# Norm sums and spreads as transposes, a down projection that ends bank by bank, and a last norm in two token halves

## The reference

```
def rmsnorm(x, g):
    y = x * lax.rsqrt(jnp.mean(x * x, axis=-1, keepdims=True) + EPS)
    return y * g
# first_block, for l in 0, 1:
    y = concat(diff_attention, spatial_gating, window_gqa)(rmsnorm(x, g_pre_mix) @ w_in) @ w_out
    x = x + rmsnorm(y, g_post_mix)
    f = (silu(h @ gate) * (h @ up)) @ w_ffn_out          # h = rmsnorm(x, g_pre_ffn)
    x = x + rmsnorm(f, g_post_ffn)
    e = p @ w_ple_up;  g = sigmoid(rmsnorm(x, g_ple_gate) @ w_ple_gate)
    x = x + rmsnorm(e * g, g_ple_post)
# second_block, for l in 0, 1:
    x = x + 0.5 * swiglu(norm(x)); x = x + mixer(norm(x)); x = x + 0.5 * swiglu(norm(x))
return norm(x)
```

## Time and profile before

| | us |
|---|---|
| median of 3 runs (3361.12 to 3364.63) | 3361.33 |
| the profiled execution, its own time | 3360.54 |
| its span in the trace | 3358.7 |
| TensorE matmul busy | 3292.1 (98%) |
| GpSimd busy | 1647.3 (49%) |
| VectorE, ScalarE busy | 1176.9, 1171.3 (35% each) |

### The profile page before, as it was taken

How to read it: one execution, slowest core, us unless ns; L and a number is a source line. 1 busy time by engine, 2 the same in 40 slices (tenths; PEclk the granted TensorE clock), 3 DMA queues, 4 the chain that set the end, 5 groups by cost and what they waited for, 6 DMA issues and landing times.

```text
span 3358.7 us, 44116 instructions
## 1 busy us (share of the span) xinstructions
PE 3292.1 (98%) x16096; PEld 2719.8 (81%) x16096; DVE 1176.9 (35%) x1850; ACT 1171.3 (35%) x1852; POOL 1647.3 (49%) x906
## 2 busy tenths in 40 slices
PE   8999999999999999999999999999999999999998
PEld 6788888787788887888888788888888887688887
DVE  4534124445441144511344332124311443321133
ACT  4744222448442233422233442223322233332232
POOL 6735444567254445644456244444544452354443
PEclk9999999999999999999999999999999999999998
DMA  4112222231122222322222112222222221122221
GB/s 151 45 47 99 94 100 94 69 110 45 38 95 100 94 100 75 117 95 99 94 88 101 51 69 93 95 96 98 97 95 99 94 95 69 63 94 94 98 96 57
DMA packets 80800, 293.87 MB, mean 87 GB/s; under 512 B 8971, under 2 KB 9355, under 8 KB 80428
## 3 DMA queue, kind: packets, MB, share of 16 engines
q1 hardware_dynamic: 79344, 286.06, 24.4%
q10 hardware_dynamic: 1340, 6.23, 0.5%
HBM read 290.15 MB, written 2.10 MB: 87 GB/s over the span
## 4 chain that ended last, share of the span: by engine, by line
PE 89%; POOL 4%; DVE 3%; issue 3%; ACT 1%; DMA 0%; POOLq 0%; SPq 0%; DVEq 0%; ACTq 0%
PE bank L1989 28%; PE bank L1991 27%; PE bank L1990 27%; POOL w_lo L559 1%; PE bank L2436 1%; POOL diag L698 1%; POOL scr L617 1%; PE bank L2397 1%; PE bank L2417 1%; PE bank L2035 1%; PE bank L2259 0%; PE bank L2017 0%; DVE y L1601 0%; PE bank L2237 0%; POOL small L611 0%
## 5 line engine op out<-in xcount | busy, mean ns | idle before, releaser
L559 POOL TENSOR_TENSOR w_lo<-w_raw,w_hi 128x1024 fp32r<-128x1024 f32 (+1 forms) x541 | 1307.4, 2420 | 1501.4 <-ACT w_hi L789 1501.2
L1989 PE MATMUL bank<-mvh,w_hi 128*128 128x512 f32 (+1 forms) x4520 | 1739.7, 385 | 31.5 <-DVE mvl L1303 14.4
L1991 PE MATMUL bank<-mvh,w_lo 128*128 128x512 f32 (+1 forms) x4520 | 1714.9, 379 | 0.0
L1990 PE MATMUL bank<-mvl,w_hi 128*128 128x512 f32 (+1 forms) x4520 | 1714.5, 379 | 0.0
L789 ACT ACTIVATE w_hi<-w_raw 128x1024 fp32r<-128x1024 f32 x537 | 568.5, 1060 | 1752.3 <-PE bank L1991 1748.7
L1989 PEld LDWEIGHTS bank<-mvh,w_hi 128*128 128x128 f32 x4520 | 851.9, 188 | 221.5 <-issue 40.5
L1991 PEld LDWEIGHTS bank<-mvh,w_lo 128*128 128x128 f32 x4520 | 851.7, 188 | 161.7
L1990 PEld LDWEIGHTS bank<-mvl,w_hi 128*128 128x128 f32 x4520 | 852.4, 189 | 152.7 <-issue 0.2
L1412 DVE TENSOR_TENSOR scr<-bank,rstd_b 128x512 f32<-128x512 f32 x264 | 181.3, 690 | 994.4 <-PE bank L1991 994.2
L1429 DVE TENSOR_TENSOR mvl<-big,mvh 128x512 fp32r<-128x512 f32 x132 | 269.3, 2050 | 347.4 <-ACT mvh L916 347.4
L698 POOL TENSOR_TENSOR diag<-diag,scr 128x512 f32<-128x512 f32 (+1 forms) x137 | 153.9, 1123 | 24.1 <-ACT scr L804 12.7
(11 more groups left out here) (195 smaller groups left out, 1565.2 us busy)
## 6 DMA issues: line engine op xcount, KB each, us to landing
w_raw<-in_weights SPq DMA_DIRECT2D x537, 512.0 KB, 3.2
x<-in_x SPq DMA_DIRECT2D x8, 256.0 KB, 8.0
out_y<-y SPq DMA_DIRECT2D x4, 512.0 KB, 2.7
tab<-in_dist ACTq DMA_DIRECT2D x2, 640.0 KB
tab<-in_gmlp ACTq DMA_DIRECT2D x2, 640.0 KB
tab<-in_ret_dil ACTq DMA_DIRECT2D x1, 1280.0 KB
y<-in_p ACTq DMA_DIRECT2D x2, 512.0 KB, 3.7
y<-in_rotary ACTq DMA_DIRECT2D x1, 1024.0 KB
```

What stands on the lines that cost most here:

```text
L559: last = nc.gpsimd.tensor_tensor(w_lo[:, slot, at], w_raw[:, slot, at], w_hi[:, slot, at].bitcast(F32), ALU.subtract)
L1989: nc.tensor.matmul(bank[:, at], hi, mvh[:, k, at], start=first, stop=False)
L1990: nc.tensor.matmul(bank[:, at], hi, mvl[:, k, at], start=False, stop=False)
L1991: return nc.tensor.matmul(bank[:, at], lo, mvh[:, k, at], start=False, stop=last)
```

## The change

Four things are changed.

1. `sum_squares` transposes the summed squares instead: four transposes of 128x128 fill bank STAT (for a half two, and two more of the last square), and DVE adds up along the free axis with a new `reduce_sum` ahead of the variance. `spread` transposes too. Each of these is one instruction for a block where there were two.
2. In `a_ffn_out` the last two units are worked bank by bank: both units' products for bank 2, then for bank 0, and so on. The norm is no longer in `DIRECT`: POOL adds all eight squares, begins with them ahead of `w_lo` of the gate's first unit, and makes that unit between the last add and the root. ACT makes `w_hi` of the last units behind the squares, and `w_hi` of the gate's third unit ahead of the first `moving_from_x` tile. The sum moves from behind the third `ple_tile` to behind the second.
3. `b_post_out1` ends bank by bank as well, and in two token halves: first all eight banks for tokens 0 to 255, then for 256 to 511 in the order of `LAST_ORDER`, with 256-column matmuls.
4. The final norm is done for each half by itself. The sum and the spread of the first half stand between matmuls of the second; y is stored in eight DMAs of 256 KB.

```diff
+LAST_ORDER = (tuple(range(8)), (1, 5, 0, 2, 3, 4, 6, 7))
...
-        DIRECT = {"final": 5}
+        DIRECT = {"final": KT - 1}
         for l in range(LAYERS):
-            DIRECT.update({f"a_out{l}": KT - 1, f"a_ffn_out{l}": KT - 1, f"a_ple{l}": KT - 1})
+            DIRECT.update({f"a_out{l}": KT - 1, f"a_ple{l}": KT - 1})
...
+        TWO_STEPS = SPLIT_POST + ["final"]
...
             return sq[:, k % 4, part(half)]
+
+        def turned(name, half):
...
-            for k in range(0, KT, 2):
-                sp.wait_ge(y_ready, k + 2)
-                sp.dma_start(y_out[:, k:k + 2, :], y[:, k:k + 2, :]).then_inc(out_stored, 16)
-            sp.wait_ge(out_stored, 16 * (KT // 2))
+            for half in range(2):
+                for k in range(0, KT, 2):
+                    sp.wait_ge(y_ready, KT * half + k + 2)
+                    sp.dma_start(y_out[:, k:k + 2, HALF[half]], y[:, k:k + 2, HALF[half]]).then_inc(out_stored, 16)
+            sp.wait_ge(out_stored, 16 * KT)
...
+                splits(u0)
+                add_squares(f"a_ffn_out{l}", 0, KT)
                 splits(u0 + 1)
-                add_squares(f"a_ffn_out{l}", 0, KT - 1)
                 root(f"a_ffn_out{l}")
                 splits(u0 + 2)
...
-            add_squares("final", 0, DIRECT["final"])
-            root("final")
+            add_squares("final", 0, KT - 1)
+            add_squares("final", KT, KT + 3)
+            root("final", 0)
+            add_squares("final", KT + 3, KT + KT - 1)
...
                     if gate and 1 <= k <= 4:
                         take_e(int(name[-1]), k + 3)
-                    if gate and k in (1, 5):
-                        after_unit(lin[f"a_ple_up{name[-1]}"], 0, k // 5)
+                    if gate and k == 5:
...
-                ffn_out(f"a_ffn_out{l}", f"a_ffn_in{l}")
+                ffn_out(f"a_ffn_out{l}", f"a_ffn_in{l}", tail=2)
...
                     square(f"a_ffn_out{l}", n, banks[BACK[n]][:, :])
+                after_unit(lin[f"a_ffn_out{l}"], 0, FT - 2)
                 after_unit(lin[f"a_ffn_out{l}"], 0, FT - 1)
                 for n in range(4):
                     take_e(l, n)
+                after_unit(lin[f"a_ple_up{l}"], 0, 0)
...
                 ffn_out(f"b_post_out{l}", f"b_post_in{l}", tail=4 if l else 0)
-            for k in range(KT):
-                act.wait_ge(x_ready, XR["b_post1"] + k + 1)
-                square("final", k, x[:, k, :])
+            for i in range(2 * KT):
+                act.wait_ge(x_ready, XR["b_post1"] + i + 1)
...
+                if turned(name, half):
+                    src = var4[:, at]
+                    if half is None:
+                        chain(nc.vector.reduce_sum(src, banks[STAT][:, :].rearrange("p (b c) -> p b c", c=P), AX.X))
+                    else:
+                        chain(nc.vector.reduce_sum(src, banks[STAT][:, :].rearrange("p (a b c) -> p b a c", a=2, c=P),
+                                                   AX.XY))
+                nc.vector.tensor_scalar(var4[:, at], src, 1.0 / D, EPS, ALU.mult, ALU.add).then_inc(var_ready, 1)
 
...
+            def last_sum(half, j):
+
+                at, k = HALF[half], LAST_ORDER[half][j]
+                dve.wait_ge(last_out, KT * half + j + 1)
+                nc.vector.scalar_tensor_tensor(out=x[:, k, at], in0=banks[BACK[k]][:, at], scalar=0.5,
+                                               in1=x[:, k, at], op0=ALU.mult, op1=ALU.add).then_inc(x_ready, 1)
+
+            def output(half, k):
+
+                at = HALF[half]
+                if k == 0:
+                    spread_ready("final", half)
+                nc.vector.scalar_tensor_tensor(out=y[:, k, at], in0=x[:, k, at], scalar=col("final", k),
+                                               in1=banks[STAT if half else BCAST][:, at], op0=ALU.mult,
+                                               op1=ALU.mult).then_inc(y_ready, 1)
+
             for k in range(KT):
-                update(k)
-            rstd_ready("final")
+                last_sum(0, k)
             for k in range(KT):
-                nc.vector.scalar_tensor_tensor(out=y[:, k, :], in0=x[:, k, :], scalar=col("final", k),
-                                               in1=banks[BCAST][:, :], op0=ALU.mult,
-                                               op1=ALU.mult).then_inc(y_ready, 1)
+                if k == 3:
+                    variance("final", 0)
+                last_sum(1, k)
+                if k == 6:
+                    output(0, 0)
+            for k in range(1, KT):
+                if k == 3:
+                    variance("final", 1)
+                output(0, k)
+            for k in range(KT):
+                output(1, k)
 
 
         @block.tensor
         def _(pe):
-            def three(bank, slot, tile, k, first, last, half=None):
+            def three(bank, slot, tile, k, first, last, half=None, again=False):
 
                 hi, lo = w_hi[:, slot, tile * P:(tile + 1) * P], w_lo[:, slot, tile * P:(tile + 1) * P]
                 at = part(half)
-                nc.tensor.matmul(bank[:, at], hi, mvh[:, k, at], start=first, stop=False)
-                nc.tensor.matmul(bank[:, at], hi, mvl[:, k, at], start=False, stop=False)
-                return nc.tensor.matmul(bank[:, at], lo, mvh[:, k, at], start=False, stop=last)
+                nc.tensor.matmul(bank[:, at], hi, mvh[:, k, at], start=first, stop=False, skip_group_check=again)
+                nc.tensor.matmul(bank[:, at], hi, mvl[:, k, at], start=False, stop=False, skip_group_check=again)
+                return nc.tensor.matmul(bank[:, at], lo, mvh[:, k, at], start=False, stop=last, skip_group_check=again)
 
             def wide(name):
...
                 pe.wait_ge(sq_used, used(name, end - (KT - first)))
+                if turned(name, half):
+                    if NORM[name] == 0:
+                        pe.wait_ge(consts, 16)
+                    for j, b in enumerate(bs):
+                        last = nc.tensor.transpose(banks[STAT][:, j * P:(j + 1) * P], diag[:, b, :], ident[:, :])
+                    if half is not None:
+                        pe.wait_ge(sq_ready, base + end)
+                        for j in range(2):
+                            last = nc.tensor.transpose(banks[STAT][:, (2 + j) * P:(3 + j) * P],
+                                                       sq_at(name, end - 1)[:, j * P:(j + 1) * P], ident[:, :])
+                    last.then_inc(sums_done, 1)
+                    return
                 for b in bs:
                     last = nc.tensor.matmul(banks[STAT][:, b:b + 1], diag[:, b, :], ones[:, 0:1], start=(b == bs[0]),
                                             stop=(first == KT), skip_group_check=True)
...
-                    last = nc.tensor.matmul(banks[STAT if half else BCAST][:, b * P:(b + 1) * P], rstd4[:, b:b + 1].broadcast_to([P, P]),
-                                            ident[:, :], start=True, stop=True)
+                    last = nc.tensor.transpose(banks[STAT if half else BCAST][:, b * P:(b + 1) * P],
+                                               rstd4[:, b:b + 1].broadcast_to([P, P]), ident[:, :])
...
                         body(t, 2 + j)
-                for f in range(FT - 4, FT):
+                if name[0] == "b" and name != "b_post_out1":
+                    for f in range(FT - 4, FT):
+                        body(0, f)
+                    return
+                for f in (FT - 4, FT - 3):
                     body(0, f)
+                pe.wait_ge(w_lo_ready, L.u0 + FT)
+                pe.wait_ge(mv_lo, L.m0 + FT)
+                if name == "b_post_out1":
+                    last_outputs(L)
+                    return
+                for n in range(8):
+                    for f in (FT - 2, FT - 1):
+                        last = three(banks[BACK[n]], (L.u0 + f) % RING, n, f % 4, False, f == FT - 1)
+                        if n == 7:
+                            last.then_inc(unit_done, 1)
+                    if n < 7:
+                        last.then_inc(out_done, 1)
+
+            def last_outputs(L):
+
+                for half in range(2):
+                    for j in range(KT):
+                        n = LAST_ORDER[half][j]
+                        if half:
+                            pe.wait_ge(x_ready, XR["b_post1"] + n + 1)
+                        for f in (FT - 2, FT - 1):
+                            last = three(banks[BACK[n]], (L.u0 + f) % RING, n, 4 + f % 4, False, f == FT - 1, half, half == 1)
+                        last.then_inc(last_out, 1)
+                        if half and j == 2:
+                            pe.wait_ge(x_ready, XR["b_post1"] + KT + 2)
+                            sum_squares("final", 0)
+                        if half and j == 5:
+                            spread("final", 0)
+                sum_squares("final", 1)
+                spread("final", 1)
 
             def ple_tile(l, n):
...
 
```

(19 more changed lines are left out.)

13 lines of the change are left out of this document (9 added, 4 removed).

## The result

| | before | after |
|---|---|---|
| median, us | 3361.22 (3360.53 to 3364.63) | 3330.07 (3328.13 to 3331.26) |
| span of the profiled execution, us | 3358.7 | 3327.3 |
| granted clock over the span | 0.995 | 0.998 |

The ratio is 0.9905, with an interval of 0.9888 to 0.9922. The forecast was 3325.9, in a range of 3318 to 3336: the gain is 31.2 us instead of 35.4.

The account below looks back on a forecast made before the run. PE was taken to bound the kernel, with pauses for POOL's sum behind a_ffn_out and a serial end. Gains of 10.4 + 2.4 + 14.0 + 8.6 = 35.4 us took 3361.33 to 3325.9, range 3318 to 3336.

Parts of the forecast that it names:

- What bounds it: Whole kernel: PE's matmuls fill 98% of the span, so a removed PE instruction is worth its length unless PE then waits.
- Part 1: Twelve full norms outside a_ffn_out: transposed sums and spreads over 512 tokens gain 10.4 us, bounds 9.0 and 10.8.
- The rival by which it turns into PE's wait everywhere: Twelve full norms and eight half steps: each 0.72 us reduction becomes a PE pause, giving 3338.7; chance 0.14 (3333 to 3341).
- Part 2: Norms in two halves, a_out and a_ple, both layers, eight half steps: gain 2.4 us, bounds 0 and 5.2.
- DVE eats all: Half steps of a_out and a_ple: the lower bound, gain 0, with DVE consuming the gain of each half.
- Part 3: Behind a_ffn_out, layers 0 and 1: the new order gains 7.5 and 6.45, 14.0 us, bounds 10.2 and 18.3.
- D: Mark behind a_ffn_out: the start of the first ple_tile, from which the forecast's steps are timed.
- R: Mark behind a_ffn_out: PE goes on with the gate's third tile, forecast 16.5 us after the first ple_tile's start.
- Half of it is clock: Behind a_ffn_out: half of the 14.0 us gain, since without a long pause no stretch runs at 1.2 GHz.
- Part 4: The end, from b_post_out1's last two units: 32.8 us becomes 24.2, gaining 8.6 us, bounds 7.1 and 9.3.
- H: Mark at the end: start of b_post_out1's last two units, from which the forecast's closing steps are timed.
- The clock: Rival at all norms: transposes lower the clock at each sum and spread, 84 us lost, 3410; chance 0.02.

Follow-up runs that it names:

- x4: The changed kernel, with DVE's reduction done twice in the 14 norms that run once, not in half steps or the last norm: 3333.46 us, ratio 0.9917.
- x3: The changed kernel, with the eight half sums of a_out and a_ple by columns of ones again, spreads still transposed: 3328.06 us, ratio 0.9899.
- x5: The changed kernel, but DVE's low_weights waits for POOL's root of the first half at a_out and a_ple, both layers: 3339.45 us, one execution.
- x8: The changed kernel, but a_ffn_out's last two units one after the other, w_hi and first w_lo placed as before the change: 3344.95 us, ratio 0.9949.

## Why the prediction was right, and the step that failed

- **What bounds it**: right. PE's own instructions were worth their length wherever nothing waited, and POOL's sum and the end held the rest.
- **Part 1**: right, 9.6 against 10.4. The narrow norms give 0.63 and not 0.8, since a spread there gets only 0.30 shorter. x4 shows that the reduction is hidden at the wide norms and exactly used up at the narrow ones. The rival by which it turns into PE's wait everywhere is refuted.
- **Part 2**: this is the step that failed: -0.9 against 2.4, and outside its own bounds, 3.3 of the 4.0 us that the trace's gain fell short. (The terms as written add up to 2.1, if the 0.3 "in all" stands for both a_ple, and to 2.4 only with 0.3 for each.) The two a_ple gain 0.2 together, near what was taken; the two a_out were to gain 1.8 and lose 1.1. I had set 0 as the lower bound, "DVE eats all". That took the reduction for a delay of 0.72 in DVE's queue, with everything else keeping its length. But POOL's root got 0.91 longer because DVE's next instruction moved ahead of it. The 0.22 for which DVE waited for ACT in before had kept the two apart. In the second half of a_out the size was wrong: I took a gain of 0.65, and it loses 0.1, since PE waits for `mvl` (0.61 at 264.83 in layer 0). The range of the whole held this miss; the mechanism of this part was wrong all the same. x3 shows the loss by taking it away; that the overlap with `low_weights` is what stretches the root is shown by x5's 0.71 at the same place.
- **Part 3**: right, each step of PE and POOL up to the spread to 0.1 us. From D: transposes done at 3.26 (3.25), `w_lo` at 5.15 (5.25), root at 6.3 (6.3), spread done at 6.8 (6.8), R at 16.8 (16.5). The variance was wrong, 5.2 and not 4.4, as it took 0.91 beside POOL's `w_lo`. By luck this cost only 0.1, because the root stood behind that same `w_lo`. "Half of it is clock" was too much: the windows of the earlier trace rows hold at most 0.28 x 12 + 0.16 x 11 = 5.1 of the 13.4. Only the way from the spread to R is 0.3 longer than taken: there are now two collisions (1.86 at 632.68, and 1.69) where there was one of 2.96. x8 shows that without the bank order nothing of it is left.
- **Part 4**: right, 9.3 against 8.6. From H: sum at 8.0 (8.0), spread at 10.9 (11), last sum at 14.3 (14.6), last y at 21.0 (21.6), end at 23.6 (24.2). The outputs (13 in 5.17, 5.2 taken) and the last DMA (2.6 from the last y to the end) were sized rightly. The 0.6 lies ahead of them: the last sum began 0.3 sooner, and from it to the first of these outputs it took 1.5 (3318.08 to 3319.58) and not 1.8.
- **The clock**: the rival is refuted. In 620 to 638, with two sets of four transposes, the granted clock is 1.00, and no fall in after's trace lies at a sum or a spread of the first 3315 us (855 to 865 has 0.83, in the attention). The Trainium skill, page "TensorE: Matmul & The Clock Gate", section "Part 4: PE-mode transpose", says that transposes don't count as PE activity in the way matmuls do; sets as short as these, between matmuls, show nothing of it in this kernel.

## What to carry to other kernels

When an added instruction on one engine is shorter than the slack, ask still what it pushes against what: a wait that it fills may have been what kept two instructions of VectorE and GpSimd apart. And a sum that has to wait for the outputs of a long accumulation is helped by letting the outputs end one by one; here this order brought 6.1 us at the end, and behind `a_ffn_out` the 13.4 us were gone without it.

## What the hardware showed beyond that

VectorE and GpSimd hold each other up with certain pairs, and then not by a part. The one that is held takes the rest of the other's time and then nearly its own, all but 0.13 to 0.19 us in these rows. DVE's `w_lo` of 1.22 took 3.42 beside POOL's of 2.39, and ended at 683.69, 1.1 behind POOL's end of 682.60. The root of 0.71 ended at 249.45, 0.6 behind DVE's end. The `mvl` of 1.69, which takes 0.74 with POOL idle, ended 0.55 behind POOL's end (637.36 and 636.81). The variance, 0.17 where POOL is idle, took 0.91 and ended with POOL's `w_lo` (625.79 and 625.77). In these four the one held had begun later; but in the earlier trace rows the `mvl` that was held began 0.03 ahead of POOL's `w_lo`. The Trainium skill, page "SBUF — State Buffer", section "SBUF: two separate sides", says that the two engines share a pair of ports, held for a whole instruction, which VectorE needs in a 2-port mode or with two SBUF inputs; these rows agree with it.

That a variance of four columns falls under it was new to me. It reads the reduction's result in SBUF. The reduction itself, which reads PSUM, kept its 0.69 beside the same `w_lo` of POOL (624.16). The old variance read PSUM as well and took 0.16, but no instruction of POOL ran beside it at any of its 23 places in before, so these runs don't show whether it would have been spared. A small instruction of this kind could have been found in before: the one of line 1828, from `small` to `small`, takes 0.17 three times and 1.09 at 2908.51, beside a `w_lo` of POOL.

The last DMA ended the span 2.5 us after its issue (3317.42 + 7.74 - 0.35 = 3324.8, span 3327.3), against 3.0 for twice the bytes in before.
